# Partners of the rotated features: small transfers inside SBUF in place of a product with a permutation

## The reference

```python
def rope_partial(x, cos, sin):
    half = ROPE_DIM // 2            # 8; ROPE_DIM is 16 of 64 features
    x1 = x[..., :half]
    x2 = x[..., half:ROPE_DIM]
    rest = x[..., ROPE_DIM:]
    return jnp.concatenate([x1 * cos - x2 * sin, x2 * cos + x1 * sin, rest], axis=-1)

def diff_mixer(h, cos, sin, w_in, lam_vecs, subln_g, w_o, lambda_init):
    q, k, v = jnp.split(h @ w_in, 3, axis=-1)
    q = rope_partial(q.reshape(B, T, H, 2, dh), cos, sin) * (dh ** -0.5)
    k = rope_partial(k.reshape(B, T, H, 2, dh), cos, sin)
    ...
    for i in range(T // Q_BLOCK):
        ...
        p = jax.nn.softmax(jnp.where(mask, s, -jnp.inf), axis=-1)
        a = p[:, :, 0] - lam * p[:, :, 1]
        outs.append(jnp.einsum('bhqk,bhkv->bhqv', a, v[:, :, :L]))
```

## Time and profile before

| | |
|---|---|
| median of 3 runs | 2382.96 us (2381.13 to 2383.39) |
| the profiled execution | 2386.98 us, span 2385.0 us |
| busy: PE, DVE, ACT, Pool | 98%, 56%, 35%, 9% of the span |
| mean granted clock of PE | 0.983 |
| moved by DMA | 288 MB, 121 GB/s |

### The profile page before, as it was taken

One profiled execution on the slowest core, in us unless ns is written; L12 is line 12 of the kernel. 1 busy time (PEld: TensorE's weight loads), 2 busy tenths in 40 slices (PEclk: granted clock), 3 DMA queues, 4 the chain that ended last, 5 costly groups with the idle time before them and its releaser, 6 DMA issues.

```text
span 2385.0 us, 28000 instructions
## 1 busy us (share of the span) xinstructions
PE 2330.1 (98%) x11346; PEld 1935.5 (81%) x11346; DVE 1338.9 (56%) x1992; ACT 835.8 (35%) x1270; POOL 215.0 (9%) x182
## 2 busy tenths in 40 slices
PE   8999999999999999999999999999999998999998
PEld 6888888877788888888788988888977767888887
DVE  7655548486239455547543566664466664644343
ACT  3322223324434322223633342322344443433221
POOL 0000004021014000003110100000121101000001
PEclk7999999999999999999999999999999999999999
DMA  8766632311212366541331256663131111443331
GB/s 316 244 202 205 198 120 79 106 37 44 62 54 71 106 203 211 195 127 41 109 98 59 63 159 222 210 211 115 43 112 54 54 45 54 143 131 96 95 101 36
DMA packets 81951, 288.09 MB, mean 121 GB/s; under 512 B 9104, under 2 KB 11280, under 8 KB 81824
## 3 DMA queue, kind: packets, MB, share of 16 engines
q1 hardware_dynamic: 81104, 284.74, 37.0%
q10 hardware_dynamic: 720, 1.57, 0.2%
HBM read 284.18 MB, written 2.10 MB: 120 GB/s over the span
## 4 chain that ended last, share of the span: by engine, by line
PE 87%; DVE 8%; ACT 3%; issue 1%; DMA 0%; POOL 0%; SPq 0%; DVEq 0%; ACTq 0%; POOLq 0%
PE bank L278 23%; PE bank L279 22%; PE bank L280 22%; DVE wlo L1512 2%; PE bank L470 1%; PE bank L423 1%; PE bank L424 1%; PE bank L402 1%; PE bank L404 1%; PE bank L403 1%; PE bank L505 1%; PE bank L428 1%; PE bank L315 1%; PE bank L316 1%; PE bank L321 1%
## 5 line engine op out<-in xcount | busy, mean ns | idle before, releaser
L1512 DVE TENSOR_TENSOR wlo<-raw,whi 128x1024 fp32r<-128x1024 f32 (+1 forms) x370 | 475.1, 1286 | 363.5 <-ACT whi L944 363.3
L278 PE MATMUL bank<-yhi,whi 128*128 128x512 f32 (+1 forms) x1672 | 655.4, 392 | 4.5 <-DVE wlo L1512 3.7
L279 PE MATMUL bank<-ylo,whi 128*128 128x512 f32 (+1 forms) x1672 | 644.9, 386 | 0.0
L280 PE MATMUL bank<-yhi,wlo 128*128 128x512 f32 (+1 forms) x1672 | 644.8, 386 | 0.0
L944 ACT ACTIVATE whi<-raw 128x1024 fp32r<-128x1024 f32 (+1 forms) x370 | 385.3, 1042 | 326.2 <-PE bank L280 253.2
L278 PEld LDWEIGHTS bank<-yhi,whi 128*128 128x128 f32 x1672 | 315.2, 189 | 85.9 <-issue 22.1
L280 PEld LDWEIGHTS bank<-yhi,wlo 128*128 128x128 f32 x1672 | 315.3, 189 | 63.3
L279 PEld LDWEIGHTS bank<-ylo,whi 128*128 128x128 f32 x1672 | 315.4, 189 | 60.3 <-issue 1.0
L278 PE MATMUL bank<-mlp_ahi,whi 128*128 128x512 f32 (+1 forms) x576 | 211.0, 366 | 0.0
L279 PE MATMUL bank<-mlp_alo,whi 128*128 128x512 f32 (+1 forms) x576 | 210.7, 366 | 0.0
L280 PE MATMUL bank<-mlp_ahi,wlo 128*128 128x512 f32 (+1 forms) x576 | 210.7, 366 | 0.0
(11 more groups left out here) (333 smaller groups left out, 2943.6 us busy)
## 6 DMA issues: line engine op xcount, KB each, us to landing
raw<-in_ada SPq DMA_DIRECT2D x152, 512.0 KB, 4.5
raw<-in_ffn_up SPq DMA_DIRECT2D x88, 512.0 KB, 4.4
raw<-in_mlp_up SPq DMA_DIRECT2D x64, 512.0 KB, 3.5
raw<-in_mlp_dn SPq DMA_DIRECT2D x64, 512.0 KB, 3.5
raw<-in_ffn_dn SPq DMA_DIRECT2D x32, 512.0 KB, 3.6
raw<-in_w_dqkv SPq DMA_DIRECT2D x24, 512.0 KB, 3.6
first<-in_ada SPq DMA_DIRECT2D x16, 512.0 KB, 15.1
raw<-in_ffn_dn SPq DMA_DIRECT2D x16, 384.0 KB, 3.7
```

The lines of the kernel that those rows point to most:

```text
L278: e.matmul(out, wh, xh, start=first, stop=False)
L279: e.matmul(out, wh, xl, start=False, stop=False)
L280: mm = e.matmul(out, wl, xh, start=False, stop=last)
L1512: e.tensor_tensor(k.wlo[:, what % NW, 0:width], raw[:, 0:width], k.f(k.whi[:, what % NW, 0:width]), ALU.subtract).then_inc(*sig.up("wlo", ...
```

## The change

The constant PERM goes, and so does PE's product with it. SP takes its place: four transfers inside SBUF for each of the 16 blocks of q and k, each 8 partitions by 512 tokens (16 KB), fetch the partners from the copy straight into dq or dk. They stand in SP's list behind the load of the unit nine ahead. Since the transfers write the rotated features only, Pool clears dq and dk once with two memsets of 128 x 4096. The sign of the lower partner moves into the sine (ACT's `scale`, from a column of constants). DVE's product takes its input from dq or dk in SBUF, in place, no longer from PSUM. DVE and Pool both wait for the transfers' semaphore (64 for four transfers), one semaphore for each of the three copy buffers. In PE's list the transposes of v (kind 2 of `turn`) stay; two products ahead of the attention's first step and all between the steps are gone. The table of constants is 520 columns wide and not 647.

```diff
-IDENT, ONES, PERM, CAUS, CNEG, INVF_C, EPS_C, HPI_C, SEL_C, NCONST = 0, 128, 256, 384, 512, 640, 641, 642, 643, 647
+IDENT, ONES, CAUS, CNEG, INVF_C, EPS_C, HPI_C, SEL_C, SIGN_C, NCONST = 0, 128, 256, 384, 512, 513, 514, 515, 519, 520
...
-            c[g + d + 8, PERM + g + d] = -1.0
-            c[g + d, PERM + g + d + 8] = 1.0
+            c[g + d, SIGN_C], c[g + d + 8, SIGN_C] = -1.0, 1.0
...
-            m = 2 * h + kind
-            out = self.bank("turn", m)
-            w.wait_ge(*sig.on("dcopy", m))
-            e.matmul(out, k.cst[:, PERM:PERM + 128], k.tm(4 + m % 3)[:, 0:S], start=True,
-                     stop=True).then_inc(*sig.up("turn", m))
-
-        for n, kt in k.d_before[0:4]:
+        for n, kt in k.d_before[0:8]:
             part(n, kt)
         turn(0)
-        turn(1)
-        for n, kt in k.d_before[4:8]:
-            part(n, kt)
-        turn(2)
-        turn(3)
         for n, kt in k.d_before[8:]:
             part(n, kt)
...
             for n in k.d_done[s - 1]:
-                turn(n)
+                if n % 3 == 2:
+                    turn(n // 3)
...
-        e.activation(k.sinr[:, :], ang, F.Sin).then_inc(*sig.up("dtrig", 0))
+        e.activation(k.sinr[:, :], ang, F.Sin, scale=k.cst[:, SIGN_C:SIGN_C + 1]).then_inc(*sig.up("dtrig", 0))
...
         def rotated(n):
             dst = (k.dk if n % 2 else k.dq)[:, n // 2, :]
-            w.wait_ge(*sig.on("turn", n))
+            w.wait_ge(k.s_swap[n % 3], 64 * (n // 3 + 1))
             w.wait_ge(*sig.on("dtrig", 0))
-            e.tensor_tensor(dst, k.banks.at("turn", n), k.sinr[:, :], ALU.mult).then_inc(
-                *sig.up("dsinm", n, bank=("turn", n)))
+            e.tensor_tensor(dst, dst, k.sinr[:, :], ALU.mult).then_inc(*sig.up("dsinm", n))
...
+        w.wait_ge(*sig.on("lin", k.last["mlp0_dn3"]))
+        e.memset(k.dq[:, :, :], 0.0).then_inc(*sig.up("dzero", 0))
+        e.memset(k.dk[:, :, :], 0.0).then_inc(*sig.up("dzero", 1))
         for n in range(16):
             x = k.tm(4 + n % 3)[:, 0:S]
             dst = (k.dk if n % 2 else k.dq)[:, n // 2, :]
-            w.wait_ge(*sig.on("turn", n))
+            w.wait_ge(k.s_swap[n % 3], 64 * (n // 3 + 1))
             w.wait_ge(*sig.on("dtrig", 2))
             e.tensor_tensor(x, x, k.cosr[:, :], ALU.mult).then_inc(*sig.up("dcosm", n))
...
+    def swap(self, m):
+
+        k, w, sig = self.k, self.w, self.sig
+        x, dst = k.tm(4 + m % 3), (k.dk if m % 2 else k.dq)[:, m // 2, :]
+        w.wait_ge(*sig.on("dzero", m % 2))
+        w.wait_ge(*sig.on("dcopy", m))
+        for g in (0, 64):
+            self.e.dma_start(dst[g:g + 8, :], x[g + 8:g + 16, 0:S]).then_inc(k.s_swap[m % 3], 16)
+            self.e.dma_start(dst[g + 8:g + 16, :], x[g:g + 8, 0:S]).then_inc(k.s_swap[m % 3], 16)
...
             e.dma_start(k.raw[:, slot, 0:width], k.dram[name][i]).then_inc(k.s_raw[slot], 16)
+            n = what - k.first["dqkv"] - 9
+            if 0 <= n < 24 and n % 3 < 2:
+                self.swap(2 * (n // 3) + n % 3)
```

More of the change, by code:

```diff
@@ L804, in part, with turn @@
                 k.banks.let_go(("u", u))
[L806 to L816, removed]
-            m = 2 * h + kind
-            out = self.bank("turn", m)
-            w.wait_ge(*sig.on("dcopy", m))
-            e.matmul(out, k.cst[:, PERM:PERM + 128], k.tm(4 + m % 3)[:, 0:S], start=True,
-                     stop=True).then_inc(*sig.up("turn", m))
-        for n, kt in k.d_before[0:4]:
+        def turn(h):
+            out = self.bank("vt", h)
+            w.wait_ge(*sig.on("vcopy", h))
+            for j in range(4):
+                c = slice(128 * j, 128 * j + 128)
+                mm = e.transpose(out[:, c], k.tm(7)[:, c], k.ident)
+            mm.then_inc(*sig.up("vt", h))
+        for n, kt in k.d_before[0:8]:
             part(n, kt)
         turn(0)
-        turn(1)
-        for n, kt in k.d_before[4:8]:
-            part(n, kt)
-        turn(2)
-        turn(3)
         for n, kt in k.d_before[8:]:
@@ L2480, in build_program @@
         k.s_first = [sem(f"s_first{n}") for n in range(NT)]
+        k.s_swap = [sem(f"s_swap{i}") for i in range(3)]
         k.s_a2, k.s_pos, k.s_c = sem("s_a2"), sem("s_pos"), sem("s_c")
```

## The result

The changed kernel takes 2394.23 us (median of 5 runs, 2393.3 to 2396.46), the kernel before 2383.09 in the same rounds: a ratio of 1.0049 with a 95% interval of 1.0038 to 1.0059. It is slower by 11.1 us, where +2.4 had been forecast.

The account below looks back on a forecast made before the run. PE and the DVE/ACT loop were both taken as near the bound. Terms -1.3 (PE) -5.0 -3.5 +12.4 (collisions) -0.2 (constants) = +2.4 us, on 2386.98 less 4.0 for the profiled run, gave 2385.4 us; range 2376 to 2394.

Parts of the forecast that it names:

- PE's saving: 16 permutation products, 13.6 us less PE work, of which 1.3 us shows, in PE-bound stretches of the attention stage.
- Rival 1: PE is the bound all through, so the whole 13.6 us comes out: 2369.4 us; chance 10%.
- The swap: Transfers on SP land 3.9 us after the conversion; DVE's later products wait 4.6 us in all, counted as 0.
- The third term: DVE's waits for the swap cost nothing, nearly all lying where DVE next waits 0.3 to 2.9 us for ACT.
- rival 2: Swaps queue behind the load's data and land 5.2 us after the conversion: +6 to +12 us more, say 2394; chance 25%.
- The collisions: DVE and Pool holding each other on SBUF in the attention loop: -5.0 and -3.5 us old, +12.4 us new.
- Term (c): New collisions of Pool's cosine product and sum with DVE work behind the sine product: +12.4 us, ends 0 and 24.
- The six conversions of (c): Steps where a conversion follows 1.8 to 2.9 us behind the sine product's start: about 1.4 us each, 8.3 us.
- The other six cases: Steps where the pair `L2205`, `L2208` follows the sine product's start at 1.4 to 1.9 us: 4.1 us.
- The three terms: Old cosine products' collisions ahead of the sine product -5.0 us, old sums' behind it -3.5, new ones +12.4.
- Small things: Pool's two memsets, shorter constants, the sine's sign and fewer PSUM banks: nothing, except 0.2 us for the constants.
- The constants' 0.2 us: Constants 65 KB shorter at the very start, which waits for transfers: up to 0.4 us gained, taken as 0.2.

Follow-up runs that it names:

- b_sbufprod: Kernel before, with DVE's sine product reading the zeroed feature tile in SBUF instead of the bank, plus Pool's two zeroings, partners left out; 2385.53 us.
- a_noswap: Changed kernel without its transfers, sine and cosine products waiting for ACT's copy and the zeroing alone, partners left out; 2384.85 us.
- v_before_comb: Kernel before, with Pool's cosine product in its own tile and released by DVE's combination of the step; 2379.3 us.
- p_noswap_comb: a_noswap with Pool's cosine product released by DVE's combination of the same step instead of by ACT's copy alone; 2375.82 us.
- f_eight: Changed kernel with each transfer cut in two by columns, eight a unit of half the bytes; 2428.5 us.
- e_two: Changed kernel with two transfers a unit instead of four, the second group's partners left out; 2390.55 us.
- z_memset: Kernel before with Pool's two zeroings and the wait for them added, nothing else; 2384.44 us.
- r_comb_late: Changed kernel with transfers ahead of the load, Pool's cosine product in its own tile released by DVE's combination, sine product behind the combination; 2381.24 us.
- q_comb: Changed kernel with transfers ahead of the load and Pool's cosine product in its own tile, released by DVE's combination of the step; 2378.62 us.
- m_poolq: Changed kernel with Pool's cosine product in its own tile, released by ACT's copy, and the four transfers issued on Pool's own queue; 2398.95 us.
- j_pool: Changed kernel with transfers ahead of the load, cosine product in its own tile released by ACT's copy, sine products of units 4 to 15 on Pool; 2387.38 us.

## Why the prediction was right and wrong

**PE's saving (-1.3 us): right as far as the noise tells.** b less a gives 0.9 us of 13.6, v less p, with Pool out of the way, 3.3; each has an interval of some 2 us on either side. PE's busy time fell by 9.8 us in the profile, less than the 14 to 19 named; its waits between 1756 and 1936 us grew from 8.5 to 21.8 us, where over 18 had been said. Rival 1 (2369.4) fell.

**The swap (0 us): this step failed.** The transfers brought 9.3 us (changed kernel less a_noswap). Two of its terms were too small. The issue pace was taken from weight loads at 0.45 us; a swap transfer takes 0.67 (+0.22, three times). The last issue to landing was taken as 1.7 us; it took 2.15. Together the landing came 4.6 us behind the conversion instead of 3.9. DVE also came to its product sooner than in the kernel before, 3.3 us behind the conversion at the median instead of 3.7. The twelve later products waited 14.6 us where 4.6 had been counted. The third and the fourth block waited 7.0 us, where 2.6 had been counted for the third and none for the fourth; they cost little of the total, since PE's first scores waited for Pool 3.1 us where they had waited 2.5.

The third term is the price of a wait. I counted it at nothing, since DVE next waits for ACT. Much of that cover is real. DVE's waits for ACT's conversion over the whole stage, in a_noswap and in the changed kernel:

```profile
DVE wlo L1499 <- ACT whi L931: 51.7, 21, 5.6
```

```profile
DVE wlo L1499 <- ACT whi L931: 41.9, 17, 5.6
```

They give back 9.8 us. DVE's waits for PE's scores fell from 10.8 to 1.2 us and those for ACT's exponentials from 11.2 to 8.8. Together that is 21.8 us, as much as the 21.6 us of new waits, and yet the stage grew by 8.8 us. By this count the loss lies in DVE's busy time, 163.5 us for 153.7, that is in the collisions with a Pool released by the landing. But a sum of waits is no path, and f_eight shows the other side: with Pool released in the same way, 31.6 us of further waits cost 34.3 us. How the 9.3 us divide between waits and collisions stays open. A run with the late landing and with Pool released by the combination would tell, and there is none.

The direction and the price are those of rival 2 (2394), which had been given 25%: issue on SP and the queue behind the load both. That its number is the measured one is in part luck, since it had the landing at 5.2 us, where it was 4.6, and left the collisions at 12.4 us. In e_two the load alone was what came last; with four transfers SP's issue was.

**The collisions (-5.0 -3.5 +12.4 = +3.9 us): right for the operands, too small for the changed kernel.** b less z gives +2.8 us, with overlapping intervals, but in b Pool's cosine product is still released by PE's product. Term (c) was laid out for a Pool released by the landing. For that case take each DVE instruction of the stage less the shortest of its shape: the excess is 10.4 us in the kernel before, 12.8 in b_sbufprod, 8.9 in a_noswap and 18.8 in the changed kernel, 8.4 more than before where 3.9 had been counted. The kinds were right: of DVE's lines behind a product, L2191 went from a mean of 0.47 to 0.63 us, five L2194 took 1.44 to 1.64, none ahead of a product did. The six conversions of (c) came to 7.4 us where 8.3 had been counted. The other six cases came to 8.6 us where 4.1 had been counted, and the third and the fourth block, which (c) left out, to 2.7.

And I tied the cost to the operands of the sine product. a_noswap and p_noswap_comb have the same operands and differ by 8.6 us, so most of it belongs to the moment at which Pool is let go. The three terms were all answers to one question, beside which DVE instruction Pool reads SBUF, and part of the old collisions could have been removed without this change (v_before_comb, 2.9 of the 8.5 us that I had put down for them).

**Small things: right.** The zeroing 0.5 us within an interval of 4 (z_memset), no wait of PE near it. The constants' 0.2 us cannot be told from the drift of the stage's start. PE's granted clock in the first stretch fell from 0.94 to 0.83, which is the lower level (1.2 GHz) for a third of it if it took only the two levels. Over the stage it is 0.95, and 0.94 both in a_noswap and in the changed kernel, so the clock is no part to speak of in the 9.3 us.

## What to carry to other kernels

Work taken off the busiest engine is worth what that engine's waits allow: look for the loop behind them first. A chain of small transfers costs its issues one after the other on the queue's engine and then waits behind whatever large transfer was issued just before; put it ahead of that load. Moving its consumer to a later place helped as long as the landing was late (8 us) and not once it was early. A second wait on an engine that waits anyway can be covered, but look also at what else the same event lets go. And where two engines exclude each other on SBUF, release the idle one by the instruction after which the busy one reads PSUM, not by its data alone: here that wait was worth 2 to 9 us (r_comb_late, v_before_comb and q_comb 2 to 3, p_noswap_comb 8.6).

## What had not been expected of the hardware

- A transfer of 8 partitions x 2 KB inside SBUF takes SP 0.62 to 0.65 us to issue, one of 8 x 1 KB the same (f_eight), a weight load of 512 KB 0.33 to 0.44. On Pool's queue the issue took 0.52 us (m_poolq). Last issue to landing is 2.0 to 2.2 us in most units with four transfers and 1.8 with eight of half the size.
- A large load held a small transfer across queues too: on Pool's queue the landing was 1.79 us behind the last issue with no load in the 8 us before it and 4.3 us with one issued on SP's queue (m_poolq).
- Pool reading SBUF holds a VectorE `TENSOR_SCALAR` of 128x2 for 0.54 us (0.71 for 0.17), and leaves a maximum of 128x512 from a bank at 0.69 us (j_pool).
- Where one landing released both, DVE's product went first (0.69 us) and Pool's paid (1.77 to 1.81 us), and then held DVE's next conversion (2.17 to 2.33 us for 1.23).
- A kernel with two transfers can be faster than the same kernel with none (2376.4 against 2384.9 us), for the moment at which they release another engine.
